# Attention ahead of the pooled branch, and the recurrence's input ahead of its gates

## What is computed

```python
# second block (one layer); h is the normalized, scaled input
u_pool, z_pool, q, k, v, z_attn, m_pool, m_attn = split(h @ w_in)
y_pool = (multiscale_pool(u_pool, w_pool_grp, pool_scale) * silu(z_pool)) @ w_pool_up
y_attn = (moba_attention(rope(q), rope(k), v) * silu(z_attn)) @ w_attn_up
merged = sigmoid(m_pool) * y_pool + sigmoid(m_attn) * y_attn
x = rms_norm(x + gate * (merged @ w_out), g_final)

# third block, mixer of each of two layers
c_gate, b_gate, v, u, g = split(h @ w_in)
y_a = b_gate * causal_conv3(c_gate * v, conv_w)
uc = causal_conv4(u, lru_conv_w) + lru_conv_b
r, i = sigmoid(uc @ wa + ba), sigmoid(uc @ wx + bx)          # block-diagonal
log_a = -8 * r * softplus(-lam)
h_t = exp(log_a) * h_(t-1) + sqrt(-expm1(2 * log_a)) * (i * uc)   # scan over the tokens
x = x + concat(y_a, h * gelu(g)) @ w_out
```

## Time and profile before

| | us |
|---|---|
| median of 3 runs | 2640.94 |
| lowest and highest | 2640.09, 2644.82 |
| the profiled execution | 2641.26 |
| its span in the trace | 2639.5 |

### The profile page before, as it was taken

How to read it: one execution, slowest core, us unless ns; L and a number is a source line. 1 busy time by engine, 2 the same in 40 slices (tenths; PEclk the granted TensorE clock), 3 DMA queues, 4 the chain that set the end, 5 groups by cost and what they waited for, 6 DMA issues and landing times.

```text
span 2639.5 us, 32770 instructions
## 1 busy us (share of the span) xinstructions
PE 2412.2 (91%) x12021; PEld 2029.7 (77%) x12021; DVE 2018.5 (76%) x1933; ACT 1429.7 (54%) x1328; POOL 17.6 (1%) x33
## 2 busy tenths in 40 slices
PE   4976999987999898788999987999999999999997
PEld 4855788875788797686888876888888888788886
DVE  6998778698687654557454575888888889888887
ACT  2543333444443444435334454777777777777775
POOL 0000000000000000000000000000000000000000
PEclk8988999998999999898999998999999999999998
DMA  8437689533579455244555534999999999999995
GB/s 321 138 125 265 225 310 325 187 125 112 177 268 339 142 188 168 80 156 133 177 189 191 162 126 156 366 334 369 333 367 334 365 334 367 334 362 340 333 366 187
DMA packets 435138, 651.78 MB, mean 247 GB/s; under 512 B 20688, under 2 KB 324432, under 8 KB 435040
## 3 DMA queue, kind: packets, MB, share of 16 engines
q1 hardware_dynamic: 432880, 643.59, 71.7%
q0 software_dynamic: 2160, 6.85, 0.8%
HBM read 649.32 MB, written 1.05 MB: 246 GB/s over the span
## 4 chain that ended last, share of the span: by engine, by line
PE 76%; DVE 15%; ACT 4%; issue 4%; DMA 1%; SPq 0%; DVEq 0%; POOL 0%; ACTq 0%
PE pair L1768 24%; PE pair L1770 23%; PE pair L1769 23%; DVE rest L960 4%; DVE aw L1293 4%; PE tb L1934 2%; ACT head L633 1%; DVE aw L979 1%; PE pair L1853 1%; PE tb L1835 1%; DMA x<-in_x 1%; ACT aw L656 1%; DVE qkv L1488 0%; DVE hT L1073 0%; DVE gat L1699 0%
## 5 line engine op out<-in xcount | busy, mean ns | idle before, releaser
L960 DVE TENSOR_TENSOR rest<-raw,head 128x2048 fp32r<-128x2048 f32 x554 | 1267.3, 2291 | 329.7 <-ACT head L633 312.9
L633 ACT ACTIVATE head<-raw 128x2048 fp32r<-128x2048 f32 x554 | 1058.5, 1912 | 362.6 <-PE pair L1770 345.3
L1768 PE MATMUL pair<-head,hTh 128*128 128x512 f32 x1968 | 800.9, 407 | 91.8 <-issue 36.5
L1769 PE MATMUL pair<-rest,hTh 128*128 128x512 f32 x1968 | 779.9, 396 | 0.0
L1770 PE MATMUL pair<-head,hTl 128*128 128x512 f32 x1968 | 779.6, 396 | 0.0
L1768 PEld LDWEIGHTS pair<-head,hTh 128*128 128x128 f32 x1968 | 377.5, 192 | 181.4 <-issue 91.6
L1770 PEld LDWEIGHTS pair<-head,hTl 128*128 128x128 f32 x1968 | 377.1, 192 | 82.0
L1769 PEld LDWEIGHTS pair<-rest,hTh 128*128 128x128 f32 x1968 | 378.5, 192 | 75.4 <-issue 1.5
L1768 PE MATMUL pair<-head,aTh 128*128 128x512 f32 x736 | 289.0, 393 | 0.0
L1770 PE MATMUL pair<-head,aTl 128*128 128x512 f32 x736 | 286.6, 389 | 0.0
L1769 PE MATMUL pair<-rest,aTh 128*128 128x512 f32 x736 | 286.5, 389 | 0.0
(11 more groups left out here) (289 smaller groups left out, 1637.0 us busy)
## 6 DMA issues: line engine op xcount, KB each, us to landing
raw<-in_moe_w_gate SPq DMA_DIRECT2D x224, 512.0 KB, 6.0
raw<-in_moe_w_up SPq DMA_DIRECT2D x224, 512.0 KB, 7.2
raw<-in_moe_w_down SPq DMA_DIRECT2D x224, 512.0 KB, 6.7
raw<-in_w_in SPq DMA_DIRECT2D x152, 512.0 KB, 4.7
raw<-in_ada_w SPq DMA_DIRECT2D x96, 512.0 KB, 5.3
raw<-in_w_ffn_in SPq DMA_DIRECT2D x88, 512.0 KB, 5.4
raw<-in_w_ffn_out SPq DMA_DIRECT2D x44, 512.0 KB, 5.5
raw<-in_w_out SPq DMA_DIRECT2D x40, 512.0 KB, 4.8
```

Source lines behind the costliest of these rows:

```text
L633: act.activation(head[:, c.split, :], raw[:, c.raw, :], ACT.Copy).then_inc(heads_done, 1)
L960: dve.tensor_tensor(rest[:, c.split, :], raw[:, c.raw, :], head[:, c.split, :].bitcast(F32), ALU.subtract).then_inc(rests_done, 1)
L1768: pe.matmul(out_, lh, rh, start=start, stop=False, skip_group_check=True)
L1769: pe.matmul(out_, lh, rl, start=False, stop=False, skip_group_check=True)
```

## The change

In the second block `q2`, `k2` and `v2` come first and the scores follow at once; `up`, `zp` and the transposes, `za` and the weighted sum come next, then the gates with the pooled product among them, then `yattn2` and `yconv2`. `apply_scores` is cut into `turn_scores` and `apply_scores`. In the mixers `uu`, `cg` and `vv` come first, the recurrence's products next, `bg` and `gg` last. In both places the features are split in two parts: the first quarter of the 1024 rows (two of eight groups of 128) goes into the spare `aTh` and `aTl`, since `hTh` and `hTl` still hold the input (`split_attn`, `rest_attn`). Some buffers move: the pooled cascade into the values' buffer, the counts into a part of `hT` (so GpSimd waits for the norm's last split before it fetches them), the recurrence's tanh into a part of `gat`.

```diff
--- before.py
+++ after.py
-    plan_linear("up", w, 512, "act", 0)
-    plan_linear("zp", w, 512, "act", 512)
     plan_linear("q2", w, 512, "act", 1024)
     plan_linear("k2", w, 512, "act", 1536)
     plan_rotate(2)
     plan_linear("v2", w, 512, "act", 2048)
-    for j in range(4):
+    plan_scores(2)
+    plan_linear("up", w, 512, "act", 0)
+    plan_linear("zp", w, 512, "act", 512)
+    plan_turns(2)
+    plan_linear("za", w, 512, "act", 2560)
+    plan.job("pv2", "act")
+    plan.split("attn2.0")
+    for j in range(2):
         plan_linear(f"gates2.{j}", w, NT, "act", 3072 + j * NT)
-    plan_linear("za", w, 512, "act", 2560)
     plan.job("pool", "dve")
+    for j in range(2, 4):
+        plan_linear(f"gates2.{j}", w, NT, "act", 3072 + j * NT)
+    plan.split("attn2.1")
     plan.split("conv2")
+    plan_linear("yattn2", a["w_attn_up_2"][0], 1024, "dve", rows=KW)
     plan_linear("yconv2", a["w_pool_up_2"][0], 1024, "dve", rows=KW)
-    plan_scores(2)
-    plan_apply(2)
-    plan.split("attn2")
-    plan_linear("yattn2", a["w_attn_up_2"][0], 1024, "dve", rows=KW)
...
-        for j, name in enumerate(("cg", "bg", "vv", "uu", "gg")):
+        for j, name in ((3, "uu"), (0, "cg"), (2, "vv")):
             plan_linear(f"{name}{l}", w, 512, "dve" if name == "vv" else "act", j * 512)
         plan.job(f"lrur{l}", "act")
         plan.job(f"lrui{l}", "act")
-        plan.split(f"lru{l}.0")
-        plan.split(f"lru{l}.1")
+        for j, name in ((1, "bg"), (4, "gg")):
+            plan_linear(f"{name}{l}", w, 512, "act", j * 512)
+        plan.split(f"ya{l}.0")
+        plan.split(f"ya{l}.1")
+        plan.split(f"yb{l}")
...
-        POOLBUF = (oT, aw[:, 0:1024].rearrange("p (g s) -> p g s", s=S))
+        POOLBUF = (qkv[:, 2, :].rearrange("p (g s) -> p g s", s=S), aw[:, 0:1024].rearrange("p (g s) -> p g s", s=S))
-        invcnt = aw[:, 2048:3072].rearrange("p (g s) -> p g s", s=S)
+        invcnt = hT[:, 4:8, :]
+        lru_t = G[:, 2060:3084].rearrange("p (g s) -> p g s", s=S)
...
             pool.wait_ge(sem("block_done"), 1)
+            pool.wait_ge(htl_ready, plan.splits["norm4.11"])
...
+            def split_attn(name, part):
+
+                act.wait_ge(sem("hT_ready"), plan.splits[f"{name}.{part}"])
+                act.activation((aTh, hTh)[part][:, 2 * part:2 * part + 2, :], hT[:, 2 * part:2 * part + 2, :], ACT.Copy).then_inc(hth_ready, 1)
...
                 for q, sc in enumerate((sc0, sc1)):
+                    if k == 2 and q == 1:
+                        feed(last_chunk("zp") + 1)
...
-            copy_job("up", upad[:, :, PADS:PADS + S])
-            copy_job("zp", xn[:, 0, :].rearrange("p (g s) -> p g s", s=S), ACT.Silu)
             copy_job("q2", qT)
             copy_job("k2", kT)
             copy_job("v2", vt, turn=False)
-            for j in range(4):
+            feed(last_chunk("up") + 2)
+            score_exps(2)
+            copy_job("up", upad[:, :, PADS:PADS + S])
+            copy_job("zp", kq[0], ACT.Silu)
+            turn_scores(2)
+            copy_job("za", kq[1], ACT.Silu)
+            apply_scores(2)
+            split_attn("attn2", 0)
+            for j in range(3):
                 gate_job(2, j)
...
+            job("gates2.3")
+            split_attn("attn2", 1)
             split("conv2", 4, 8)
+            gate_job(2, 3)
...
+                feed(last_chunk(f"gg{l}") + 1)
                 act.wait_ge(sem("b_square"), l + 1)
-                act.activation(aw4[2], aw4[2], ACT.Sqrt, scale=-1.0).then_inc(sem("b_root"), 1)
-                split(f"lru{l}.1", 4, 8)
+                act.activation(lru_t, lru_t, ACT.Sqrt, scale=-1.0).then_inc(sem("b_root"), 1)
+                copy_job(f"bg{l}", kq[1])
+                split_attn(f"ya{l}", 0)
+                job(f"gg{l}")
+                act.activation(kq[2], flat4(bank(f"gg{l}")), ACT.Gelu_apprx_tanh).then_inc(evac["act"], 1)
+                split_attn(f"ya{l}", 1)
+                split(f"yb{l}", 4, 8)
...
+            for name in ("zp", "za"):
+                feed(last_chunk(name) + 1 + AHEAD)
+            dve.wait_ge(evac["act"], plan.jobs["pv2"][4])
+            did(dve.tensor_tensor(hT[:, 0:4, :], oT[:, :, :], kq[1], ALU.mult))
+            now()
+            dve.sem_inc(sem("hT_ready"), 1)
+            rest_attn("attn2", 0)
...
-            def linear(name, cols, k0=0, turn=False, splits=()):
+            def linear(name, cols, turn=False, splits=(), k0=0, attn=None):
...
+                            if attn and j == 0 and kk in (0, 2):
+                                ready(f"{attn}.{kk // 2}")
...
-                                    ins = three(ps[:, t, :], hTh[:, kk, toks], hTl[:, kk, toks],
+                                    h_, l_ = (aTh, aTl) if attn and kk < 2 else (hTh, hTl)
+                                    ins = three(ps[:, t, :], h_[:, kk, toks], l_[:, kk, toks],
```

More of the change, by code:

```diff
@@ L1033, in split_rest, with rest_attn @@
                 dve.tensor_tensor(hTl[:, lo:hi, :], hT[:, lo:hi, :], hTh[:, lo:hi, :].bitcast(F32),
+                                  ALU.subtract).then_inc(htl_ready, 1)
+            def rest_attn(name, part):
+                ks = slice(2 * part, 2 * part + 2)
+                dve.wait_ge(hth_ready, plan.splits[f"{name}.{part}"])
+                dve.tensor_tensor((aTl, hTl)[part][:, ks, :], hT[:, ks, :], (aTh, hTh)[part][:, ks, :].bitcast(F32),
                                   ALU.subtract).then_inc(htl_ready, 1)
@@ L1541, in _ @@
             dve.sem_inc(sem("pool_ready"), 1)
[L1542 to L1543 removed]
+            feed(last_chunk("gates2.1") + 1 + AHEAD)
             dve.wait_ge(job_done, jobs_done("pool"))
@@ L1813, in linear_by_tiles @@
                             kk, wcols = 4 * ch + k, slice(k * NT, (k + 1) * NT)
-                            ins = three(ps[:, t, :], hTh[:, kk, toks], hTl[:, kk, toks], head[:, c.split, wcols], rest[:, c.split, wcols],
+                            h_, l_ = (aTh, aTl) if attn and kk < 2 else (hTh, hTl)
+                            ins = three(ps[:, t, :], h_[:, kk, toks], l_[:, kk, toks], head[:, c.split, wcols], rest[:, c.split, wcols],
                                         kk == 0, kk == 7)
@@ L2055, in _ @@
                 ffn(*DENSE[l], 2 * l + 1)
-            linear("up", 512, turn=True, splits=("norm4.10", "norm4.11"))
-            for name in ("zp", "q2", "k2"):
-                linear(name, 512, turn=True)
+            linear("q2", 512, turn=True, splits=("norm4.10", "norm4.11"))
+            linear("k2", 512, turn=True)
             rotate(2)
             linear("v2", 512)
-            for j in range(4):
-                linear(f"gates2.{j}", NT)
+            scores(2)
+            linear("up", 512, turn=True)
+            linear("zp", 512, turn=True)
+            turn_scores(2)
             linear("za", 512, turn=True)
+            apply_scores(2)
+            linear("gates2.0", NT)
+            linear("gates2.1", NT)
             pe.wait_ge(sem("pool_ready"), 1)
@@ L2070, in _ @@
             ins.then_inc(job_done, 1)
+            linear("gates2.2", NT)
+            linear("gates2.3", NT)
+            linear("yattn2", D, attn="attn2")
             linear("yconv2", D, k0=4, splits=("conv2",))
-            scores(2)
-            apply_scores(2)
-            linear("yattn2", D, splits=("attn2",))
             mix(2)
@@ L2078, in _ @@
             for l in range(2):
-                for name in ("cg", "bg", "vv", "uu", "gg"):
-                    linear(f"{name}{l}", 512, turn=True, splits=(f"norm{5 + 2 * l}.10", f"norm{5 + 2 * l}.11") if name == "cg" else ())
+                for name in ("uu", "cg", "vv"):
+                    linear(f"{name}{l}", 512, turn=True, splits=(f"norm{5 + 2 * l}.10", f"norm{5 + 2 * l}.11") if name == "uu" else ())
                 pe.wait_ge(sem("uc_ready"), l + 1)
```

124 lines of the change are left out of this document (62 added, 62 removed).

## The result

| | before | changed |
|---|---|---|
| median, us | 2642.86 (4 runs, 2640.09 to 2644.82) | 2594.23 (4 runs, 2592.92 to 2596.41) |
| span of the profiled execution, us | 2639.5 | 2594.6 |

The ratio is 0.9818, with a 95% interval of 0.9801 to 0.9835: 48.6 us less by the medians, 44.9 by the spans. The forecast was 2597.5. Nine further runs of the kernel before, taken with the experiments, have a median of 2640.07; against them the gain is 45.8 us, the better figure, since the four runs of the table scatter by 4.7.

The account below looks back on a forecast made before the run. PE, busy 91%, was taken to bound the kernel, its pauses and slow clock being what could change. The block's 26.2 us and two mixers' 17.6 gave 43.8, from 2641.3 to 2597.5; forecast 2593 to 2601 (72%), low end 2590, high end 2608.

Parts of the forecast that it names:

- 27.2 us gone: Second block: PE's pauses of 20.75 us, 4.1 of slow clock in yconv and yattn, and 2.4 of slow transposes go.
- the new pause of 1.00: Second block, ahead of up: PE waits for the bank of the first scores, a new pause of 1.0 us.
- Softmax under `up` and `zp`: Second block: up and zp cover the softmax, 24.7 us of work ending within 26.9, 2 us to spare.
- The first rest for `gates2.1`: Second block, VectorE behind the weighted sum: 9.8 us of steps against 10.8 for gates2.0, fits by 1.0.
- the chain ahead of gelu: Each mixer: ScalarE loads gelu's table by 26.2 us, gg ends at 26.6, so the recurrence is covered by 0.4.
- The first rest of the output weights: Each mixer: this VectorE step is done at 25.3 us, before gg ends at 26.6, covered by 1.3.
- 2.0 back in pieces: Each mixer, behind gg: a pause of 2.0 us in pieces replaces 9.38, after 12 and 24 output projection matmuls.
- a fall in the pieces: Each mixer, behind gg: the clock falls in the short pauses, taken as 1.7 us, bounds 0 and 3.1.
- ScalarE last in the mixers: Rival, mixers: costlier table switches or a late head make ScalarE end last, 4.3 us in each, 2606; 10%.
- The starved gates: Rival, second block: the wait for the weighted sum starves gates2.1 and followers, 2601.5, or 2606 with pooled matmuls late; 12%.
- the clock stays low: Rival, reordered stretches: the new mix or short pauses keep the clock at its lower level, 2715 if throughout; 3%.
- the pause only moves: Rival, mixers: the pause shifts from before the output projection to before gg, only the block's 26.2 remain, 2615; 3%.

Follow-up runs that it names:

- e8: Changed kernel with e4's edit, and in the second block the head ahead of the scores' copies placed behind them, VectorE's feed moved to match: 2589.22 us, ratio 0.9805.
- e5: Changed kernel with one more table switch (a one-column exponential) on ScalarE ahead of gg's heads in each mixer: 2597.49 us, ratio 0.9835.
- e7: Changed kernel with three copies of 1024 elements added on VectorE between the attention's first split and the cascade in the second block: 2593.32 us, ratio 0.982.
- e3: Changed kernel without the spare buffers in the mixers, all features split into hTh and hTl after gg: 2603.34 us, ratio 0.986.
- e2: Changed kernel with the second block put back to the old order, both recurrent mixers in the new one: 2619.05 us, ratio 0.992.
- e4: Changed kernel with gelu's table loaded before gg's end, the second split and rest ahead of gelu, next weight rests ahead of the wait for gelu: 2592.13 us, ratio 0.9816.
- e1: Changed kernel with both recurrent mixers put back to the old order, the second block in the new one: 2613.97 us, ratio 0.990.
- e6: Changed kernel with three more table switches (exp, sqrt, exp of one column) on ScalarE ahead of gg's heads in each mixer: 2601.87 us, ratio 0.9855.

## Why the prediction was right

**What the block lost.** Predicted 27.2 us gone (pauses 20.75, clock 4.1, transposes 2.4) and 1.0 new; measured 27.24 net, with the new pause of 1.00 at its place and with its cause: the head between the copy of v2 and the scores' copies, as e8 shows. The net is 1.0 over the 26.2 predicted. Most of it is the clock at the block's start. The first 24 us, two projections in either kernel, before:

```profile
911.76:935.70 23.94, 23.94 (x187) 23.94 (x188) 14.56 (x12) 10.38 (x7) 1.29 (x2) 0.93 0.61 209
```

and in the changed kernel:

```profile
914.08:938.00 23.92, 23.54 (x193) 23.35 (x194) 14.48 (x12) 9.10 (x7) 1.29 (x2) 1.00 0.62 211
```

The granted clock is 0.93 in one and 1.00 in the other. e5 has the new block with the clock at 0.93 in the same place, and there it takes 150.52, 0.9 more than the 149.64 (it has the slow clock in place of the pause of 0.38): against that start the change is worth 26.4 us. This stretch follows the first block and its norm, which the change doesn't touch. The transposes at 1.03 per 8 are the price taken from the earlier trace rows.

**The covers.** Softmax under `up` and `zp`: no pause, and with more to spare than the 2 us predicted. VectorE's last division ends at 971.9, 7.4 us ahead of the transposes; the sum had put ScalarE's two heads and VectorE's two rests one behind the other, where the engines work side by side. The first rest for `gates2.1`: slack 1.0 predicted, 1.3 by the trace, 1.1 by e7. In the mixers the chain ahead of gelu: 0.4 predicted, 0.89 by the trace and by e5. The first rest of the output weights ends at 1168.82 + 2.29 = 1171.1, 1.5 ahead of PE's start at 1172.58, where 1.3 was predicted. The spare buffers cost nothing and hid what they were said to hide (e3).

**The mixers.** 12.5 us gone, 2.0 back in pieces: 1.8 measured, the pieces where they were expected, behind 12 and 24 matmuls. The term that was mis-sized is the clock: 1.7 us were taken for a fall in the pieces, and it was 0 (granted clock 1.00 in both windows above, and no slow stretch there in either mixer of e2, e5 or e7). So a mixer brought 10.3 instead of 8.8 (12.5 less 1.8 would be 10.7; 0.3 of the other 0.4 is the price of the 84 matmuls, taken as 18.9 us, where e4 has 1524.07 - 1504.86 = 19.2 without a pause). The bound of 0 had been named; the value was taken from the row "with split pauses like these", in the mixing step, where the pauses are 1.70 and 0.72. The same code with the same two pauses in the changed kernel:

```profile
1068.08:1073.08 5.00, 4.82 (x21) 4.03 (x22) 2.85 (x3) 3.39 (x3) 0.00 (x0) 1.00 0.01 3
```

The clock is 1.00 there, where it was 0.66. Of the ten profiles it fell in this place in three (before, e5, e7). So the row was one execution's luck, taken as the price, and it stood for longer pauses than the pieces turned out to be.

**The rest of the sum.** 27.2 + 20.4 = 47.6 us by the stages that were changed, where 43.8 had been forecast. The span fell by 44.9 only, because start, tail and the stages between came out 2.7 longer on balance (+2.3, +2.5, -0.5, -1.6). The prediction had the experts' part keep its length; whether the 2.5 of the tail are scatter is open, as said above. By the medians the gain is 45.8, 2.0 over the forecast. The other 1.2 of the 3.3 us by which 2597.5 was too high lie in the starting point: the forecast was taken from a profiled execution of 2641.3, and the kernel before has a median of 2640.1. The clock's term in two mixers alone, 3.4, is more than the 2.0. So the mechanism was right, and the closeness of the number is in part luck: of the 3.8 us by which the changed stages brought more than forecast, 1.8 do not appear in the medians, and why is open. The medians of e1 and e2 are the cleaner measure of the parts: 26.1 against 26.2 for the block, 21.0 against 17.6 for the mixers.

**The rivals.** ScalarE last in the mixers did not occur; e5 shows what it would take and what it would cost, 0.6 us in each mixer for a delay of 1.5, and e6 3.6 for 4.5, the latter with a fall of the clock. The starved gates did not occur; a delay of 2.2 costs 1.1. That the clock stays low did not occur: 8 transposes took 1.03. That the pause only moves is excluded by e2.

## What to carry to other kernels

A pause of the bounding engine is best removed by giving it work that nothing waits for, and the price is then read from the slack at the few places where the covered chain meets it again: here 0.9, 1.1 to 1.3 and 1.5 us, the first two confirmed by a small delay put in on purpose. What is left after such a reordering is often no dependency but a step's place in an in-order queue: moving a split, a table load, some rests and a head took out all three pieces that the large change had left in these places. Do not price the slow clock by one row of one execution. Here it fell behind every pause of over 3 us in the mixers and behind none of the pieces under 0.9, and in between (2.27, or 1.70 and 0.72 close together) in some profiles only, so such a pause is priced as a chance. Cutting a pause of 3.80 us into 0.48 and 0.80 saved the clock as well as the pause; it made each pause shorter and their sum too, and which of the two counts was not tried apart.
